# Expert rows weighted on leaving PSUM and summed in DRAM by an accumulating scatter; gate/up of the last expert ahead of down of 30

## What is computed

```python
def hierarchical_moe(x, ...):
    g_gate, g_idx = lax.top_k(softmax(x @ w_group + b_group), 1)      # one of 4 groups
    e_gate, e_idx = lax.top_k(softmax(logits of that group's 8 experts), 2)
    e_gate = e_gate / sum(e_gate)
    combine = one_hot(e_idx) * e_gate * g_gate
    y = sum over 32 experts e:  (silu(x @ w_gate[e]) * (x @ w_up[e]) * combine[:, e]) @ w_down[e]

h = layer_norm(alpha * x + mixer(x))
out = layer_norm(alpha * h + hierarchical_moe(h))
```

## Time and profile before

| | us |
|---|---|
| median of 3 runs | 577.28 (576.37 to 580.02) |
| the profiled execution, device time | 580.89 |
| its span, first to last instruction | 579.2 |
| granted TensorE clock, mean of the span | 0.949 |
| TensorE matmuls busy | 506.2 (87%) |
| DVE busy | 248.4 (43%) |
| ACT busy | 184.8 (32%) |
| GpSimd busy | 149.1 (26%) |
| DMA moved | 144.12 MB, 134.40 on SP's queue, 9.18 on GpSimd's |

### The profile page before, as it was taken

How to read it: one execution, slowest core, us unless ns; L and a number is a source line. 1 busy time by engine, 2 the same in 40 slices (tenths; PEclk the granted TensorE clock), 3 DMA queues, 4 the chain that set the end, 5 groups by cost and what they waited for, 6 DMA issues and landing times.

```text
span 579.2 us, 8049 instructions
## 1 busy us (share of the span) xinstructions
PE 506.2 (87%) x3064; PEld 334.9 (58%) x3064; DVE 248.4 (43%) x466; ACT 184.8 (32%) x377; POOL 149.1 (26%) x129
## 2 busy tenths in 40 slices
PE   4999999999999996799854899999997897777683
PEld 3888766766676664588653555555554454445231
DVE  2400266696776655400656443332332222225167
ACT  3312255554554553223422122322222212211132
POOL 3444345364231221044001121222121111201000
PEclk9999999999999997799975899999999988999798
DMA  6423221952112124168995799999999999999633
GB/s 244 157 76 106 78 68 38 368 116 72 37 44 66 37 74 176 79 220 323 396 382 200 292 373 417 415 416 414 416 415 416 416 416 418 413 418 405 235 154 145
DMA packets 53239, 144.12 MB, mean 249 GB/s; under 512 B 11014, under 2 KB 27414, under 8 KB 45008
## 3 DMA queue, kind: packets, MB, share of 16 engines
q1 hardware_dynamic: 48160, 134.40, 60.4%
q0 software_dynamic: 5040, 9.18, 4.4%
HBM read 135.45 MB, written 16.27 MB: 262 GB/s over the span
## 4 chain that ended last, share of the span: by engine, by line
PE 34%; DMA 10%; SPq 5%; DVE 5%; issue 3%; ACT 0%; POOLq 0%; DVEq 0%
PE bank L1461 14%; PE bank L1488 7%; DMA gate_w<-in_w_gate 4%; DMA down_w<-in_w_down 4%; SPq L373 2%; PE bank L1448 2%; PE bank L1255 2%; PE bank L1257 2%; PE bank L1256 2%; DMA xe<-h_rows,idx_all 2%; SPq L370 1%; SPq L376 1%; PE bank L1403 1%; PE bank L1474 1%; PE bank L1463 1%
## 5 line engine op out<-in xcount | busy, mean ns | idle before, releaser
L1461 PE MATMUL bank<-gate_w,xeT 128*64 128x256 f32 x512 | 125.7, 402 | 20.7 <-issue 19.0
L1463 PE MATMUL bank<-up_w,xeT 128*64 128x256 f32 x512 | 126.0, 403 | 0.0
L502 POOL TENSOR_TENSOR w_lo<-raw,w_hi 128x1024 fp32r<-128x1024 f32 x32 | 80.6, 2520 | 131.0 <-ACT w_hi L616 130.8
L1461 PEld LDWEIGHTS bank<-gate_w,xeT 128*64 128x64 f32 x512 | 71.8, 145 | 57.0 <-issue 26.2
L1463 PEld LDWEIGHTS bank<-up_w,xeT 128*64 128x64 f32 x512 | 71.8, 145 | 0.0
L1488 PE MATMUL bank<-down_w,hidT 128*64 128x512 f32 x256 | 63.1, 614 | 5.1 <-DMA down_w<-in_w_down 4.6
L1070 DVE TENSOR_TENSOR silu_hid<-silu_hid,bank 64x256 f32<-64x256 f32 x32 | 13.5, 423 | 119.5 <-ACT silu_hid L750 119.4
L750 ACT ACTIVATE silu_hid<-bank 64x256 f32<-64x256 f32 x32 | 12.1, 377 | 132.5 <-PE bank L1463 132.5
L1255 PE MATMUL bank<-xT_hi,w_hi 128*128 128x512 f32 x128 | 53.6, 418 | 0.8 <-ACT values L635 0.8
L616 ACT ACTIVATE w_hi<-raw 128x1024 fp32r<-128x1024 f32 x32 | 33.8, 1057 | 62.1 <-PE bank L1257 47.8
L1257 PE MATMUL bank<-xT_lo,w_hi 128*128 128x512 f32 x128 | 50.7, 396 | 0.0
(11 more groups left out here) (170 smaller groups left out, 804.4 us busy)
## 6 DMA issues: line engine op xcount, KB each, us to landing
gate_w<-in_w_gate SPq DMA_DIRECT2D x32, 1024.0 KB, 24.2
up_w<-in_w_up SPq DMA_DIRECT2D x32, 1024.0 KB, 25.1
down_w<-in_w_down SPq DMA_DIRECT2D x32, 1024.0 KB, 24.4
raw<-in_w_in SPq DMA_DIRECT2D x24, 512.0 KB, 3.9
expert_rows<-xe SPq DMA_DIRECT2D x1, 4096.0 KB, 15.0
raw<-in_w_out SPq DMA_DIRECT2D x8, 512.0 KB, 3.4
hx<-in_x SPq DMA_DIRECT2D x4, 512.0 KB, 5.4
h_rows<-hx SPq DMA_DIRECT2D x4, 512.0 KB, 11.6
```

Of the source, the lines that this page charges most:

```text
L502: nc.gpsimd.tensor_tensor(w_lo[:, slot, :], raw[:, slot, :], w_hi[:, slot, :].bitcast(F32), ALU.subtract).then_inc(s_lo, 1)
L1461: nc.tensor.matmul(GATE[h], xeT[:, m % 2, c, half(h)], gate_w[r][:, c, :], start=(c == 0), stop=(c == KD - 1))
L1463: mm = nc.tensor.matmul(UP[h], xeT[:, m % 2, c, half(h)], up_w[r][:, c, :], start=(c == 0), stop=(c == KD - 1))
```

## The change

Six things change.

1. `expert_rows` has 512 rows, one a token. `idx_all` has one column a pair, for gather and scatter alike.
2. `put(e)` adds to the rows in DRAM (`compute_op=ALU.add`) instead of writing them. Two experts may hold the same token, so `put(e)` now waits until `put(e - 1)` has landed (`s_put[1 - h]`).
3. The gate is applied when the rows leave PSUM: L758 gets `scale=slot_gate`, L1086 becomes a multiply by it. `slot_gate` comes from a second half of `slots`: sixteen more small matmuls with the gates in place of token numbers, after `gate` is known (`s_gated`), and a DVE copy (`s_slotgate`). DVE waits for it before the loop.
4. The end reads one row a token: four loads instead of eight. `other_rows`, the five diagonals, `last_gate` and `second_y` go. `add_first` is an addition for all four tiles, all ahead of `add_rest(0)`.
5. The exception for e = 30 goes on TensorE, ACT and DVE: `gate_up(31)` stands ahead of `down(30)`.
6. The zeros are 2 MB instead of 4 MB.

```diff
-    y_dram = nc.dram_tensor("expert_rows", [2 * S, D], F32).ap()
+    y_dram = nc.dram_tensor("expert_rows", [S, D], F32).ap()
...
             def put(e):
                 m, h = e // 2, e % 2
                 pool.wait_ge(s_ya, e + 1)
                 pool.wait_ge(s_yd, e + 1)
+                if e >= 1:
+                    pool.wait_ge(s_put[1 - h], 16 * ((e - 1) // 2) + 16)
                 pool.indirect_dma_start(
...
-                    in_=y_rows[half(h), :], in_offset=None, bounds_check=2 * S - 1,
-                    oob_is_err=False).then_inc(s_put[h], 16)
+                    in_=y_rows[half(h), :], in_offset=None, bounds_check=S - 1,
+                    oob_is_err=False, compute_op=ALU.add).then_inc(s_put[h], 16)
...
-                nc.scalar.activation(y_rows[half(h), 0:D // 2], DN[h][0], ACT.Copy).then_inc(s_ya, 1)
+                nc.scalar.activation(y_rows[half(h), 0:D // 2], DN[h][0], ACT.Copy,
+                                     scale=slot_gate[half(h), e // 2:e // 2 + 1]).then_inc(s_ya, 1)
...
-                nc.vector.tensor_copy(y_rows[half(h), D // 2:], DN[h][1]).then_inc(s_yd, 1)
+                nc.vector.tensor_scalar(y_rows[half(h), D // 2:], DN[h][1], slot_gate[half(h), e // 2:e // 2 + 1], None,
+                                        ALU.mult).then_inc(s_yd, 1)
...
             for t in range(T):
-                sp.dma_start(first_y[:, t, :], y_v[:, 0, t, :]).then_inc(s_first[t], 16)
-                sp.dma_start(second_y[:, t, :], y_v[:, 1, t, :]).then_inc(s_first[t], 16)
+                sp.dma_start(first_y[:, t, :], y_v[:, t, :]).then_inc(s_first[t], 16)
...
+            def slot_gates(ps):
+
+                dve.wait_ge(s_weighted, ps + 1)
+                nc.vector.tensor_copy(slot_gate[:, :], bank[:, 3, 0:MOE_PAIRS]).then_inc(s_slotgate, 1)
...
+            nc.vector.tensor_tensor(ids_at[:, :, 1, :], chosen[:, :, :, :].rearrange("p k t e -> p (k t) e"),
+                                    gate[:, :, :].rearrange("p k t -> p (k t)").unsqueeze(2).broadcast_to([P, 2 * T, E]),
+                                    ALU.mult).then_inc(s_gated, 1)
+            slot_gates(0)
...
+            dve.wait_ge(s_slotgate, 1)
             n_passes = dve.value_load(passes_i[0:1, 0:1], min_val=1, max_val=S // SLOTS)
...
             def add_first(t):
-                dve.wait_ge(s_first[t], 32)
-                nc.vector.scalar_tensor_tensor(out=hx[:, t, :], in0=first_y[:, t, :], scalar=gate[:, 0, t:t + 1],
-                                               in1=hx[:, t, :], op0=ALU.mult, op1=ALU.add).then_inc(s_res1, 1)
+                dve.wait_ge(s_first[t], 16)
+                nc.vector.tensor_tensor(hx[:, t, :], first_y[:, t, :], hx[:, t, :], ALU.add).then_inc(s_res1, 1)
...
-            add_first(0)
-            add_first(1)
+            for t in range(T):
+                add_first(t)
             add_rest(0)
-            add_rest(1)
-            finished(0)
-            add_first(T - 1)
-            for t in range(2, T):
+            for t in range(1, T):
                 add_rest(t)
                 finished(t - 1)
             finished(T - 1)
...
             def slots(ps):
 
                 pe.wait_ge(s_slots, ps + 1)
-                for j in range(2 * T):
-                    for h in range(2):
-                        mm = nc.tensor.matmul(bank[half(h), 7, 0:E].rearrange("p (c m) -> p c m", c=2),
-                                              at_rank[:, j, :], ids_at[:, j, :, h::2],
-                                              start=(j == 0), stop=(j == 2 * T - 1))
-                mm.then_inc(s_slotted, 1)
+                for c in range(2):
+                    if c == 1 and isinstance(ps, int):
+                        pe.wait_ge(s_gated, 1)
+                    for j in range(2 * T):
+                        for h in range(2):
+                            mm = nc.tensor.matmul(bank[half(h), (7, 3)[c], 0:MOE_PAIRS],
+                                                  at_rank[:, j, :], ids_at[:, j, c, h::2],
+                                                  start=(j == 0), stop=(j == 2 * T - 1))
+                    mm.then_inc(s_slotted if c == 0 else s_weighted, 1)
...
             for e in range(1, E):
-                if e == E - 2:
-                    down(e)
                 if e + 1 < E:
                     gate_up(e + 1)
...
-                if e != E - 2:
-                    down(e)
+                down(e)
...
                 for j in range(2):
-                    nc.tensor.matmul(bank[:, b + j, :], place_T[:, t, :], y_rows[:, j * 512:(j + 1) * 512],
-                                     start=True, stop=False)
+                    mm = nc.tensor.matmul(bank[:, b + j, :], place_T[:, t, :], y_rows[:, j * 512:(j + 1) * 512],
+                                          start=True, stop=True)
-            def other_rows(t):
...
                 mm.then_inc(s_last, 1)
```

More of the change, by code:

```diff
@@ L168, in build @@
         iota_i = sb("iota_i", [P, SLOTS], I32)
-        ids_i = sb("ids_i", [P, 2, T, 2], I32)
+        ids_i = sb("ids_i", [P, 2, T], I32)
         top[0] = arena + (RING - 1) * SLOT
         idx_get = sb("idx_get", [P, 1], I32)
-        idx_put = sb("idx_put", [P, 1], I32)
-        empty = sb("empty", [P, 2, MOE_PAIRS])
+        idx_put = sb("idx_put", [P, 2], I32)
+        empty = sb("empty", [P, MOE_PAIRS])
         xe_off = attention_end
@@ L580, in _ @@
                         pool.nop(nofuse=True)
[L581 to L586, removed]
+                        for h in range(2):
+                            pool.indirect_dma_start(
+                                out=y_dram, out_offset=bass.IndirectOffsetOnAxis(ap=idx_put[half(0), h:h + 1], axis=0),
+                                in_=y_rows[half(h), :], in_offset=None, bounds_check=S - 1,
+                                oob_is_err=False, compute_op=ALU.add).then_inc(x_put, 16)
+                            pool.wait_ge(x_put, 32 * c - 16 + 16 * h)
+                            pool.nop(nofuse=True)
                 pool.sem_inc(x_go, 1)
-                pool.wait_ge(s_idx, n_passes + 1)
+                pool.wait_ge(s_odd, n_passes + 1)
                 pool.nop(nofuse=True)
@@ L771, in _ @@
                             act.nop(nofuse=True)
-                            nc.scalar.activation(y_rows[half(h), 0:D // 2], DN[h][0], ACT.Copy).then_inc(x_ya, 1)
+                            nc.scalar.activation(y_rows[half(h), 0:D // 2], DN[h][0], ACT.Copy,
+                                                 scale=slot_gate[half(h), ds(m, 1)]).then_inc(x_ya, 1)
             with act.Else():
@@ L778, in _ @@
             silu(1)
+            act.wait_ge(s_slotgate, 1)
             turned_half(1)
@@ L1160, in _ @@
                             dve.nop(nofuse=True)
-                            nc.vector.tensor_copy(y_rows[half(h), D // 2:], DN[h][1]).then_inc(x_yd, 1)
+                            nc.vector.tensor_scalar(y_rows[half(h), D // 2:], DN[h][1], slot_gate[half(h), ds(m, 1)], None,
+                                                    ALU.mult).then_inc(x_yd, 1)
                 dve.wait_ge(x_go, n_passes)
@@ L1169, in _ @@
                 fill_slots(n_passes)
+                slot_gates(n_passes)
             with dve.Else():
@@ L1570, in last_rows @@
                 for j in range(2):
-                    nc.tensor.matmul(bank[:, b + j, :], place_T[:, t, :], y_rows[:, j * 512:(j + 1) * 512],
-                                     start=True, stop=False)
-            def other_rows(t):
-                b = 2 * (T - 1 - t)
-                pe.wait_ge(s_first[t], 32)
-                if t == BY_PE:
-                    for j in range(2):
-                        nc.tensor.matmul(bank[:, b + j, :], first_diag[:, :], first_y[:, t, j * 512:(j + 1) * 512],
-                                         start=False, stop=False)
-                for j in range(2):
-                    mm = nc.tensor.matmul(bank[:, b + j, :], gate_diag[:, t, :], second_y[:, t, j * 512:(j + 1) * 512],
-                                          start=False, stop=True)
+                    mm = nc.tensor.matmul(bank[:, b + j, :], place_T[:, t, :], y_rows[:, j * 512:(j + 1) * 512],
+                                          start=True, stop=True)
                 mm.then_inc(s_last, 1)
```

78 lines of the change are left out of this document (30 added, 48 removed).

## The result

The changed kernel took 604.82 us (median of 4 runs, 599.95 to 607.7) against 577.15 (median of 4): 1.046 times as long, 95% interval 1.037 to 1.055. Beside the experiments it was run again: 598.51 us (median of 5), ratio 1.036, 1.032 to 1.040. It is slower by 21 to 28 us. The prediction was 604, range 583 to 636.

What follows compares the result with a forecast made beforehand. Weight bytes over 418 GB/s set the expert stage's end; the change makes the chain of puts later. Put 29 at 571.4, then landing, loads and tail give span 605.4, 26.2 us more: 577.3 + 26.2 = 603.5, predicted 604 us, range 583 to 636.

Steps and rivals of the forecast that it cites:

- The serial wait: Expert stage: put e starts only after put e - 1 landed; plain-put interval 6.5 + 0.8 = 7.3 us.
- The price of the add: An accumulating put's extra read adds 1.2 us an interval, between 0 and 3.2: 8.5 us under loads, 6.0 behind.
- The length of the chain: Put 0 at 333.7 to put 29 at 571.4 us: 25.6 puts at 8.5 us, 3.4 at 6.0.
- The bytes: Second reads add 9.4 us of DMA time in the expert stage; not added to the later chain of puts.
- The start: Before the first put, DVE waits for the second half of slots: 0.8 us later, bounds 0 and 1.0.
- The tail: Behind put 29's landing: four loads 8.1 us, last addition 1.3, norm 16.2 and waits 0.1, store 3.1.
- Order and copies: End of expert stage: the order saves about 6 us by itself, 0 under late puts; scaled copies add 0.
- Bytes only: Rival: the add costs 0.3 us a put, interval 7.6, 584 us; chance 0.21 for bytes only or less.
- the serial one: Rival: each put reads, then writes, one after the other, 3.2 us a put; 649 us, chance 0.15.
- the puts do not bind: Rival: puts land within 6.27 us, add included, and their bytes are free; 571 us, chance 0.07.
- the idle DMA shares: Sign of a wrong forecast: DMA shares clearly under 1.0 before 520 us, meaning read and write run in sequence.
- The granted clock: Sign of a wrong forecast: TensorE's clock at 0.5 in the expert stage, its 6.2 us an expert nearing the interval.

Runs made afterwards that it cites:

- wait_only: The kernel before plus one wait: put e waits for the landing of put e - 1, puts still write; 584.29 us, ratio 1.015.
- no_add: The changed kernel with the addition left out of the puts, which overwrite instead; 576.65 us, ratio 0.999.
- add_only: The kernel before with the addition alone: every put adds to its own zeroed row, no put waits for another; 588.89 us, ratio 1.017.
- old_order: The changed kernel with part 5 undone, down of 30 ahead of gate/up of 31; 600.04 us, ratio 1.036.
- two_halves: The changed kernel without the serial wait: even and odd experts add into separate halves of expert_rows, eight loads back; 595.09 us, ratio 1.034.
- order_only: The kernel before with part 5 alone, gate/up of 31 ahead of down of 30; 574.70 us, ratio 0.995.

## Why the prediction was right, step by step

**The serial wait.** Right in kind and size. Handoff: 0.8 us expected, 0.8 to 0.9 seen. Interval of plain puts: 7.3 expected, 7.51 and 7.26 measured (wait_only, no_add). The wait alone costs 1.5%, the add alone 1.7%. With the wait in place the same add costs more: from no_add to the changed kernel it is 22 us (576.65 to 598.51), from before to add_only 11 (577.8 or 578.2 to 588.89), because the 24 links from put 1 to put 25 are longer by 25 us together, of which the last four, no longer beside loads, win back 4 (23.8 us against 27.7), while without a chain only the DMA time counts.

**The price of the add.** 1.2 us a put was taken between 0 and 3.2; it is 1.05 by no_add and 0.80 by wait_only. The mechanism was told in part only: I had thought of the row's read, but GpSimd's issue also grew, from 0.90 to 1.44 us, which no row of before could show. The chosen comparison of gather and put said 0.2 us without load and 1.8 with it; the traces give 0.8 to 1.0 with load and about 1.0 without. That a value between those two came near is in part luck.

**The length of the chain.** The stretch from put 0 to put 29 was 231.1 us (342.01 to 573.10) where 237.7 (333.7 to 571.4) was predicted, 6.6 us too long. Most of that is the interval beside the loads: the first 25 took 207.3 us, 8.3 each, where 8.5 each makes 212.5, so 5.2 us. The last four took 23.8 us where 25.2 were left by the sum, 1.4 us less, though the term behind it was further off: I took 4.0 + 1.2 us for a landing with DMA empty, from the first put. A plain put lands there in 2.5 to 2.6 (once in 3.5) and an adding one in 3.6. The first put of the earlier trace rows had more beside it than the prediction said: the DMA share was 1.06 between 332 and 336 us, and its issue took 1.37 us instead of 0.90. So the last two intervals were 5.1 and 4.5 instead of 6.0, while the one before them, 6.4, was not yet free of loads.

**The bytes.** 9.4 us of DMA time: 11.5 by the queue table (37.0 against 25.5 us of all sixteen engines), 10.7 by put 29 of add_only. As predicted it did not add up with the chain. The Trainium skill says ("Collectives: The Full Stack", "The bandwidth ceiling: the fold count and why AG ≠ RS ≠ AR") that an add costs its second read and no cycles. For the time of the DMA engines this case agrees in size, 0.38 us a put by the table where the second read alone is 0.31 by bytes; the link in the chain grew by more, 0.80 to 1.05 us.

**The start.** 0.8 us more expected between first gather and first put, at most 1.0; 25.3 us (316.75 to 342.01) against 24.2 (308.69 to 332.89) is 1.1, and no_add and old_order have 1.2 and 1.3. The 8.1 us ahead of the gather were not foreseen, and in most executions they seem absent: six of nine take 597 to 602 us. That 604 was met so closely is therefore luck: two of the four executions behind that median have spans of 605.4 and 606.0 us, for which the prediction had no term, and the chain that I made 6.6 us too long is an error of the opposite sign. The prediction for an undisturbed start should have been 597 or 598, against 598.51 measured the second time.

**The tail.** From the start of put 29 to DVE's last instruction 30.9 us expected, 29.8 measured (573.10 to 602.90): the landing was 1.6 us shorter (3.6 for 5.2), the four loads 0.6 longer (8.7 for 8.1).

**Order and copies.** Part 5: 0 expected and 0 found in the changed kernel; by itself the last copies came 4.2 us nearer to put 29 where 6 were expected, and the medians differ by 3.5. The scaled copies cost DVE 0.76 instead of 0.69 us, inside the wait, as bounded. Parts 1, 3 and 6 were not run by themselves; what shows them small is no_add, which has them all and takes the time of before.

**The rivals.** Bytes only (584 us) was excluded by the 0.80 to 1.05 us, against its 0.3; the serial one by the same numbers, against its 3.2; "the puts do not bind" by the intervals, and wait_only shows that even plain puts bind. Of the signs named in advance, the idle DMA shares did not come: the shares stayed at 1.02. TensorE's idle times began at 382 us instead of 340. The granted clock did fall to 0.50 behind some of them, to 0.92 over 350 to 530 us where before had 1.00 and 0.94, but the handoffs of 0.8 to 0.9 us show that the puts never waited for it.

## What to carry to other kernels

In this kernel a scatter that waits for the one before it costs its whole landing, about 7 us beside a full DMA, even if it carries 128 KB; multiply landing plus handoff by the number of links and compare that with the stage before merging two outputs into one accumulated row. An accumulating scatter pays on three accounts: issue time on GpSimd, DMA time, and the order that it forces. When one of them is taken away, look at what comes back in the tail: two_halves won 18 us in the chain and lost 8 to its second set of loads. And when work is moved ahead of a wait, look also at what the clock did behind that wait: in order_only the same eight matmuls took 1.72 us instead of 3.68.

## What was not expected of the hardware

- An accumulating scatter of 64 slots takes GpSimd 1.42 to 1.46 us to issue, a plain one of the same shape 0.90 to 0.93 (the first of each execution 1.91 and 1.37).
- Its landing is 0.8 to 1.0 us longer beside full DMA (medians 7.3, against 6.5 and 6.3) and about 1.0 alone (3.6, against 2.5 and 2.6; one plain put took 3.5).
- With no_add, DMA moved 422 GB/s in the full stretch where before and wait_only moved 416, and an interval took 7.26 us against wait_only's 7.51. Its plain writes go to 512 rows instead of 1024, and some overwrite one another; whether that is the cause was not tried.
- TensorE's granted clock fell to 0.5 from about 286 or 288 us on in two of the five profiles with the changed routing, and only from about 296 in the other three. Their first gathers came at 316.75 and 314.68 us instead of 307.05 to 308.79.
